# Post norms of a two-block transformer kernel: weights multiplied in ahead of the rms, x and the scaled product in one operation, last squares read from the banks

## Reference

```
def rms_norm(x, gain):
    xf = x.astype(jnp.float32)
    y = xf * lax.rsqrt(jnp.mean(xf * xf, axis=-1, keepdims=True) + NORM_EPS)
    return (y * gain.astype(jnp.float32)).astype(x.dtype)

    y = jnp.concatenate([ya, yb, yc], axis=-1) @ w_out      # hybrid_layer, twice
    return x + rms_norm(y, g_post)
...
    mix = (g_lru * y_lru + g_attn * y_attn) @ w_out[l].astype(dt)
    x = x + rms_norm_2(mix, post_mix_norm[l])

    h = rms_norm_2(x, pre_ffn_norm[l])
    f = (jax.nn.silu(h @ w_ffn_gate[l].astype(dt)) * (h @ w_ffn_up[l].astype(dt))) @ w_ffn_down[l].astype(dt)
    x = x + rms_norm_2(f, post_ffn_norm[l])
```

## Time and profile before

| | us |
|---|---|
| median of 3 runs | 1973.49 |
| lowest and highest run | 1972.63, 1975.47 |
| the profiled execution, its own time | 1973.32 |
| its span, first to last instruction | 1971.5 |
| TensorE busy, share of the span | 1888.8, 96% |
| VectorE busy | 779.6, 40% |
| ScalarE busy | 876.6, 44% |
| GpSimd busy | 662.5, 34% |

### The profile page before, as it was taken

How to read it: one execution, slowest core, us unless ns; L and a number is a source line. 1 busy time by engine, 2 the same in 40 slices (tenths; PEclk the granted TensorE clock), 3 DMA queues, 4 the chain that set the end, 5 groups by cost and what they waited for, 6 DMA issues and landing times.

```text
span 1971.5 us, 24056 instructions
## 1 busy us (share of the span) xinstructions
PE 1888.8 (96%) x9233; PEld 1539.2 (78%) x9239; DVE 779.6 (40%) x1346; ACT 876.6 (44%) x1727; POOL 662.5 (34%) x278
## 2 busy tenths in 40 slices
PE   7998999899999899989899999999999999999998
PEld 6887787777788678777677888888788878888886
DVE  3435656535444465644645752011350441111002
ACT  4555565544445546555434723333443353233222
POOL 2432233123242233222223544334104424443442
PEclk9999999999999999999999999999999999999999
DMA  4321222212331122211332222222102423222222
GB/s 155 107 64 54 86 75 86 65 51 107 115 111 66 49 80 86 86 54 54 118 128 75 97 97 88 94 86 96 44 1 88 141 73 99 98 100 97 97 97 85
DMA packets 48411, 170.06 MB, mean 86 GB/s; under 512 B 6960, under 2 KB 7216, under 8 KB 47664
## 3 DMA queue, kind: packets, MB, share of 16 engines
q1 hardware_dynamic: 46480, 154.95, 23.9%
q10 hardware_dynamic: 1824, 13.63, 1.8%
HBM read 155.97 MB, written 6.29 MB: 82 GB/s over the span
## 4 chain that ended last, share of the span: by engine, by line
PE 83%; DVE 10%; ACT 4%; issue 3%; DMA 0%; POOL 0%; DVEq 0%; ACTq 0%; POOLq 0%
PE bank L670 13%; PE bank L672 13%; PE bank L671 13%; PE bank L673 10%; PE bank L675 10%; PE bank L674 10%; PE bank L797 2%; PE bank L814 2%; PE bank L775 1%; PE bank L773 1%; PE bank L776 1%; DVE y_tok L1423 1%; PE bank L761 1%; PE bank L828 1%; PE bank L827 1%
## 5 line engine op out<-in xcount | busy, mean ns | idle before, releaser
L653 POOL TENSOR_TENSOR w_hl<-w_raw,w_hl 128x1024 fp32r<-128x1024 f32 x274 | 662.3, 2421 | 1284.6 <-ACT w_hl L925 1284.1
L925 ACT ACTIVATE w_hl<-w_raw 128x1024 fp32r<-128x1024 f32 x274 | 287.7, 1058 | 346.8 <-DMA w_raw<-wstream 346.0
L670 PE MATMUL bank<-act_hl,w_hl 128*128 128x512 f32 x1056 | 427.0, 404 | 3.1 <-DVE act_hl L1296 1.9
L672 PE MATMUL bank<-act_hl,w_hl 128*128 128x512 f32 x1056 | 414.6, 393 | 0.0
L671 PE MATMUL bank<-act_hl,w_hl 128*128 128x512 f32 x1056 | 413.9, 392 | 0.0
L673 PE MATMUL bank<-w_hl,act_hl 128*128 128x512 f32 x672 | 265.8, 396 | 4.7 <-POOL w_hl L653 2.3
L675 PE MATMUL bank<-w_hl,act_hl 128*128 128x512 f32 x672 | 262.4, 390 | 0.0
L674 PE MATMUL bank<-w_hl,act_hl 128*128 128x512 f32 x672 | 262.2, 390 | 0.0
L670 PEld LDWEIGHTS bank<-act_hl,w_hl 128*128 128x128 f32 x1056 | 200.4, 190 | 45.3 <-issue 3.9
L672 PEld LDWEIGHTS bank<-act_hl,w_hl 128*128 128x128 f32 x1056 | 199.8, 189 | 43.4
L671 PEld LDWEIGHTS bank<-act_hl,w_hl 128*128 128x128 f32 x1056 | 200.4, 190 | 40.7 <-issue 2.2
(11 more groups left out here) (231 smaller groups left out, 2798.8 us busy)
## 6 DMA issues: line engine op xcount, KB each, us to landing
w_raw<-wstream SPq DMA_DIRECT2D x274, 512.0 KB, 3.4
q_dup<-q_dup SPq DMA_DIRECT2D x48, 128.0 KB, 3.7
x_spill<-x_res ACTq DMA_DIRECT2D x2, 2048.0 KB, 6.9
x_res<-x_spill ACTq DMA_DIRECT2D x2, 2048.0 KB, 8.3
x_res<-x SPq DMA_DIRECT2D x4, 512.0 KB, 6.4
g_post<-post_gains ACTq DMA_DIRECT2D x4, 512.0 KB, 3.7
x_res<-x ACTq DMA_DIRECT2D x1, 2048.0 KB, 8.4
out<-x_res SPq DMA_DIRECT2D x4, 512.0 KB, 2.6
```

The costliest lines, as they stand in the source:

```text
L653: nc.gpsimd.tensor_tensor(w_hl[:, slot, 1].rearrange("p c n -> p (c n)"), w_raw[:, slot, :], w_hl[:, slot, 0].rearrange("p c n -> p (c n)" ...
L670: pe.matmul(out_ap, wh, ah, start=start, stop=False)
L672: return pe.matmul(out_ap, wl, ah, start=False, stop=stop)
L925: nc.scalar.activation(w_hl[:, b % RING, 0].rearrange("p c n -> p (c n)"), w_raw[:, b % RING, :], ACT.Copy).then_inc(s_high_done, 1)
```

## The change

In post(i) VectorE multiplies the first halves of all four tiles with g_post ahead of everything else, as soon as ScalarE has their squares (a new semaphore half_squares). The second half of each tile is multiplied with g_post when it comes: in posts 0 and 1 after the drain, from y_acc into a slot of probs; in posts 2 and 3 straight from the bank into y, with no drain, but after ScalarE has read the squares of that bank (a new semaphore squared, one signal per tile). In posts 2 and 3 ScalarE therefore squares from the bank and waits for the matmuls, not for a drain. Then x_res = y * scale + x_res is one scalar_tensor_tensor: two of 512 columns in posts 0 and 1, one of 1024 in post 2, two of 512 with a signal each in post 3. The final store goes in eight halves of 256 KB instead of four pieces of 512 KB.

```diff
@@ SyncE, the store
             for t in range(TT):
-                sp.wait_ge(s_x_new, 3 * TT + t + 1)
-                sp.dma_start(out.rearrange("b (t p) d -> p (b t) d", p=P)[:, t, :], x_res[:, t, :]).then_inc(s_stored, 16)
-            sp.wait_ge(s_stored, 16 * TT)
+                for m in range(2):
+                    sp.wait_ge(s_x_new, 3 * TT + 2 * t + m + 1)
+                    cols = slice(m * D // 2, (m + 1) * D // 2)
+                    sp.dma_start(out.rearrange("b (t p) d -> p (b t) d", p=P)[:, t, cols], x_res[:, t, cols])\
+                        .then_inc(s_stored, 16)
+            sp.wait_ge(s_stored, 2 * 16 * TT)
@@ ScalarE
-            def row_scale(src, t, at_, first=None):
+            def row_scale(src, t, at_, first=None, squared=None):
...
-                lo = 0 if first is None else D // 2
-                link(nc.scalar.activation(probs[:, 0:2, :].rearrange("p a s -> p (a s)")[:, lo:D], src[:, t, lo:D],
+                link(nc.scalar.activation(probs[:, 0:2, :].rearrange("p a s -> p (a s)")[:, 0:src.shape[-1]], src,
                                           ACT.Square, accum_out=stat[:, at_ + t:at_ + t + 1]))
+                if squared is not None:
+                    act.sem_inc(squared, 1)
...
                 link(nc.scalar.activation(stat[:, 44:48], stat[:, 40:44], ACT.Identity, bias=eps[:, 0:1], scale=1.0 / D))
+                act.sem_inc(s_half_squares, 1)
...
                 for t in range(TT):
-                    act.wait_ge(*drained(("dense", LAST[i], t)))
-                    row_scale(y, t, 20, stat[:, 44 + t:45 + t]).then_inc(s_y_scale, 1)
+                    if i >= 2:
+                        act.wait_ge(*tile_full(LAST[i], t))
+                        half, squared = bank[t][:, :], s_squared
+                    else:
+                        act.wait_ge(*drained(("dense", LAST[i], t)))
+                        half, squared = y_acc[:, t, D // 2:D], None
+                    row_scale(half, t, 20, stat[:, 44 + t:45 + t], squared).then_inc(s_y_scale, 1)
                     if i < 3 and t > 0:
                         norm_row(i + 1, t - 1)
@@ VectorE, post(i)
                 y = y_ffn if i == 3 else y_acc
+                one, two = slice(0, D // 2), slice(D // 2, D)
                 dve.wait_ge(s_gain_in, 16 * (i + 1))
+                dve.wait_ge(s_half_squares, i + 1)
+                for t in range(TT):
+                    link(nc.vector.tensor_tensor(y[:, t, one], y[:, t, one], g_post[:, one], ALU.mult))
+
+                def with_gain(t):
+                    if i >= 2:
+                        dve.wait_ge(s_squared, (i - 2) * TT + t + 1)
+                        link(nc.vector.tensor_tensor(y[:, t, two], bank[t][:, :], g_post[:, two], ALU.mult))
+                        dve.sem_inc(freed(("dense", LAST[i], t)), 1)
+                    else:
+                        drain(LAST[i], range(t, t + 1))
+                        dve.wait_ge(*drained(("dense", LAST[i], t)))
+                        link(nc.vector.tensor_tensor(probs[:, 2 + t % 2, :], y[:, t, two], g_post[:, two], ALU.mult))
+
+                def scaled(t, cols, src):
+                    return nc.vector.scalar_tensor_tensor(out=x_res[:, t, cols], in0=src, scalar=stat[:, 28 + t:29 + t],
+                                                          in1=x_res[:, t, cols], op0=ALU.mult, op1=ALU.add)
+
+                with_gain(0)
                 if i < 3:
                     dve.wait_ge(s_x_back, 16 * (i + 1))
-                drain(LAST[i], range(1))
                 for t in range(TT):
                     if t + 1 < TT:
-                        drain(LAST[i], range(t + 1, t + 2))
+                        with_gain(t + 1)
                     dve.wait_ge(s_y_scale, i * TT + t + 1)
-                    link(nc.vector.scalar_tensor_tensor(out=y[:, t, :], in0=y[:, t, :], scalar=stat[:, 28 + t:29 + t],
-                                                        in1=g_post[:, :], op0=ALU.mult, op1=ALU.mult))
-                    nc.vector.tensor_tensor(x_res[:, t, :], x_res[:, t, :], y[:, t, :], ALU.add).then_inc(s_x_new, 1)
+                    if i == 2:
+                        scaled(t, slice(0, D), y[:, t, :]).then_inc(s_x_new, 1)
+                    elif i == 3:
+                        scaled(t, one, y[:, t, one]).then_inc(s_x_new, 1)
+                        scaled(t, two, y[:, t, two]).then_inc(s_x_new, 1)
+                    else:
+                        link(scaled(t, one, y[:, t, one]))
+                        scaled(t, two, probs[:, 2 + t % 2, :]).then_inc(s_x_new, 1)
                     if i < 3 and t > 0:
                         norm_row(i + 1, t - 1)
```

More of the change, by code:

```diff
@@ L449, in build @@
     s_y_scale = nc.alloc_semaphore("y_scale")
+    s_half_squares = nc.alloc_semaphore("half_squares")
+    s_squared = nc.alloc_semaphore("squared")
     s_setup = nc.alloc_semaphore("setup")
@@ L944, in norm_row @@
                     act.wait_ge(s_x_new, (i - 1) * TT + t + 1)
-                row_scale(x_res, t, 0).then_inc(s_h_scale, 1)
+                row_scale(x_res[:, t, :], t, 0).then_inc(s_h_scale, 1)
             def norm(i):
@@ L1174, in first_half @@
                 link(nc.scalar.activation(stat[:, 44:48], stat[:, 40:44], ACT.Identity, bias=eps[:, 0:1], scale=1.0 / D))
+                act.sem_inc(s_half_squares, 1)
             def post(i):
-                y = y_ffn if i == 3 else y_acc
                 if i >= 2:
```

## The result

| | us |
|---|---|
| changed kernel, median of 6 runs (lowest, highest) | 1980.72 (1978.87, 1982.95) |
| kernel before, median of 6 runs | 1974.53 |
| ratio, with its 95% interval | 1.003 (1.002 to 1.0041) |
| profiled execution, its span | 1978.0 against 1971.5 |

The change costs 6.2 us (4 to 8 by the interval). To compare stages between executions I use a mark that doesn't depend on where a stage begins: the time from the start of the last dense matmul ahead of a post to the start of t3's turns against the diagonal. For post 3 it is the time from the start of the last matmul to the end of VectorE's last operation ("x done"), and from there to the end of the span. A span is given to 0.1 us, so an end mark can be 0.05 off.

A forecast was written before the change was run, and what follows sets the result against it. TensorE holds 83% of the chain, but in a post's stage VectorE is the bound with ScalarE close behind. Terms against 1973.32 us: 2 x 3.25 + 3.8 - 2.7 = +7.6, giving 1980.9 us, range 1976 to 1983.5.

The forecast's parts named there:

- the clock in post 2: Post 2: TensorE's clock falls in the 2.3 us idle before t1's turns, adding 1.5 us (bounds 0 and 2.1).
- Posts 0 and 1: Each of these two stages gets 3.25 us longer: 2.75 from VectorE's delayed work and 0.5 from TensorE's clock.
- GpSimd, H2, GpSimd, H3: Posts 0 and 1: GpSimd's two weight blocks alternate with VectorE's third and fourth first-half products, which end at 490.35.
- Rival (b): Posts 0 and 1: VectorE finishes all first-half products before GpSimd; +2.4 us, 1975.7; chance 0.13 together with another rival.
- (c): Posts 0 and 1: no GpSimd block stands in the first-half products' way; -3.5 us, 1969.8; chance 0.04.
- The clock in posts 0 and 1: TensorE idles 3.9 us before t0's turns; if its clock falls, 0.5 us stays in each stage.
- rival (d): TensorE's clock stays low through one whole stage; +4.7 us on the forecast, 1985.6; chance 0.09.
- the ring: Post 2: x row, squares, second-half product and x wait on each other, 4.4 us a turn against 3.2; +2.3 us.
- after 2.23 us it fell: TensorE: after idle times of 2.23 and 4.53 us the granted clock was 0.50 in the next 2 us.
- case (a): As the forecast, but TensorE's clock holds in the three gaps; +5.1 us, 1978.4; chance 0.26.
- Post 3 and the store: At the end x is done 2.05 us sooner and the halved last store saves 0.65 us, together -2.7.
- Covered at nothing: The two new semaphores, SP's waits, GpSimd's delayed blocks and later bank frees were taken to cost nothing.

The follow-up runs named there:

- e5: Changed kernel, but in posts 0 and 1 ScalarE makes the second weight block's high part behind the post, leaving GpSimd one block; 1973.24 us, ratio 0.999.
- e6: Changed kernel, but in posts 0 and 1 the four first-half products take one input from a bank instead of y; 1971.04 us, a single run.
- e7: Changed kernel with 27 filler matmuls instead of 10 ahead of the first turns of posts 0 and 1; 1978.36 us, ratio 1.0019.
- e4: Changed kernel, but in post 2 ScalarE squares tile t+1 ahead of the x row of t-1; 1976.17 us, ratio 1.0005.
- e2: Kernel before with the new form in post 2 only; 1976.31 us, ratio 1.0005.
- e8: Changed kernel with the final store in four whole tiles again; 1979.05 us, a single run.
- e3: Kernel before with the new form in post 3 and the store in halves only; 1970.03 us, ratio 0.9978.
- e1: Kernel before with the new form in posts 0 and 1 only; 1979.44 us, ratio 1.0028.

## Why the prediction was right, and where not

The time (1980.9 against 1980.72), the sign and the range held, and most of the mechanism with them. That the time is met to 0.2 us is luck: the loss was forecast at 7.6 us over 1973.32 and measured at 6.2 over 1974.53, so a loss 1.4 too large and a baseline 1.2 too low cancel. The loss was too large mainly because one term was, the clock in post 2.

- **Posts 0 and 1, 3.25 each.** Measured 3.00 and 3.03. The step "GpSimd, H2, GpSimd, H3" is shown: 7.03 us for the four products, 5.37 for the pair; e5 takes one turn of the alternation away and 2.08 us with it, e6 takes the shared input away and all of it. x of t0 was done 3.04 us after the last dense matmul's start (496.75 less 493.71); the step had 3.2 (494.8 less 491.58). Rival (b), that VectorE gets through first, and (c), that GpSimd is absent, are refuted by the same rows. What the new form would cost in posts 0 and 1 with no block of GpSimd in the way (-1.7 by the prediction) no run shows; the sum under (c) is also wrong in itself, since 2 x -1.7 + 2.3 - 2.7 is -3.8 and not -3.5.
- **The clock in posts 0 and 1, 0.5 each.** Shown by e7, worth 0.6. It fell in both, and rose again within the stage (t3's turns take 1.05 us as before), so rival (d), a whole stage at the lower clock, is out.
- **Post 2, 2.3 for the ring and 1.5 for the clock.** The ring is shown, size 2.34 by the mark, and opened by e4. The clock term failed: TensorE idled 2.22 us ahead of t1 as computed (2.3), and the granted clock behind it stayed 1.00. The step that failed took "after 2.23 us it fell" for a rule about that length. Six profiles have this idle time of 2.22 us in post 2 (the changed kernel, e2, e5, e6, e7, e8), and the clock fell in none of them; behind the 2.23 us near 162, the row that the step rests on, it fell in 10 of 13. Post 2 came out as case (a), posts 0 and 1 as the full forecast.
- **Post 3 and the store, -2.05 and -0.65.** Measured -1.91 and -0.59 (e3, e8). Most of the 0.14 lies in a signal: from the last bank product to the next x 0.84 us pass where I had 0.73 (last section).
- **The sum.** By marks +5.9 for 7.6, of which post 2 is 1.5. The 0.3 between +5.9 and the measured 6.2 us are within the interval of the ratio.
- **"Covered at nothing"** held for the waits: none of SyncE, of a weight block or of a bank appeared in place of the removed ones. It did not hold for s_squared, which was to be a signal only: it costs about 0.1 us on the way each time (last section).

## What to carry to other kernels

Work moved into an engine's idle time costs nothing only if the thing it shares is idle too: here VectorE was free and what it shares with GpSimd, the way to SBUF for a second input, was not, and what stood queued behind the stalled products paid for it. Before a new wait on another engine goes ahead of an instruction, look at what that engine does between its signals: one row in the wrong order made a ring that cost more than the saved copies brought, and swapping the rows turned +2.3 into -1.9. Measure such edits stage by stage with a mark inside the execution, since 2 us of another stage's clock can hide or double them.

## What the runs showed of the hardware that I had not expected

**The same idle gap, two clocks.** Long before the first post, in code that the change doesn't touch, TensorE idles 3.42 us. In the execution of before the clock held behind it; in that of the changed kernel, at 181.46, it was 0.50:

```profile
181.46 1.12 PE L854 MATMUL bank<-ident,y_tok 128*128 128x128 f32 x4 [3.42 <-DVE y_tok L1518]
```
```profile
182.00:184.00 2.00, 2.00 (x11) 0.50 0.04 8
```

From this gap to the first dense matmul of the next part (201.03 before, 202.57 after) the two executions take 18.84 and 21.11 us, 2.27 apart. The row of before was the rarer case: the clock fell at this gap in 11 of the 13 profiled executions. Around 1030, behind an idle time of 2.12 us, it was the other way round, 0.72 before and 1.00 after, first before, then after:

```profile
1026.00:1032.00 6.00, 5.92 (x15) 0.72 0.13 51
```
```profile
1035.00:1041.00 6.00, 6.00 (x24) 1.00 0.05 18
```

Behind the eight idle times of 3.7 us ahead of t0's turns (posts 0 and 1 of the changed kernel, e1, e4 and e8) it fell every time. Over all profiled executions the last dense matmul ahead of post(0) starts between 490.25 and 493.90, though the program is nearly the same up to there. The same shows in the unprofiled executions: of 71 of the kernel before, the 25 with a mean granted clock of 0.989 have a median of 1976.3 us, the nine with 0.992 one of 1973.0. So the medians scatter against the marks with the clock. Why e3's executions drew the higher one stays open.

**A signal of its own costs 0.1 us on the way.** In post 2 a separate signal stands between the bank product and x: x starts 0.85 after the product (1590.03, 1590.88), in post 0, without it, 0.72 (495.21 after 494.49). That the product reads a bank is not the reason: e6's four, without such a signal, take 2.87 us, 0.73 from one to the next.

**How two engines share when both are always ready.** Neither keeps its turn: once GpSimd was there, block, product, block, product followed each other, though VectorE's next instruction stood ready 0.03 us after the last. The Trainium skill (SBUF — State Buffer, SBUF: two separate sides) has the exclusion for a whole instruction, which these rows agree with: the third product ended at 489.48, 0.55 us after the first block. The turns are what this case adds.
